# Gates of half of the tokens through an indirect scatter into DRAM, in place of one-hot products, and four more early chunks

## The chip, the cores and the metric

One core of one Trainium2 chip. The metric is the device time of one execution in microseconds, as the median of three runs.

## The reference

Two transformer-like blocks over 256 tokens of width 1024, all in float32. The change touches the last stage of the second block only, a product-key expert layer (`_peer`):

```python
q = (tok @ w_q).reshape(n_tok, 8, 2, 128)
s = jnp.einsum('nhpc,hpkc->nhpk', q, sub_keys)            # 8 heads, 2 halves, 128 keys
s_top, i_top = lax.top_k(s, 16)
cand = (s_top[:, :, 0, :, None] + s_top[:, :, 1, None, :]).reshape(n_tok, 8, 256)
best, pos = lax.top_k(cand, 16)
expert = ...                                              # i_top[.., 0, ..] * 128 + i_top[.., 1, ..] at pos
gate = jax.nn.softmax(best, axis=-1)
act = gelu(einsum('tkd,td->tk', u_emb[expert], tok)) * gate
out = einsum('tk,tkd->td', act, v_emb[expert])
```

There are 16384 experts, 128 x 128, and each token picks 128 of them (8 heads, 16 each; one expert can be picked by several heads, and its gates add up). The kernel doesn't gather: it computes the products with all experts and multiplies by a gate that is zero where an expert was not picked.

## The kernel before

Weights stream from HBM through a ring of four slots (`ring`, 512 KB each), loaded by SP. For float32 accuracy each weight chunk and each activation is kept as a high and a low part; ACT makes the high part (`take_hi`, `mid_hi`), DVE or POOL the low part (`take_lo`), and PE does three products (high x high, high x low, low x high; `TERMS`).

The expert layer (`peer`) takes the 16384 experts as 128 chunks of 128. A chunk is one second-half key j with all 128 first-half keys i on the partitions. `gate_map` [128, 128 chunks, 256 tokens] holds for each chunk gelu(u . token), later times the gate.

- Scores: PE multiplies queries by sub-keys for both token blocks of 128 (L3125). DVE then searches the two blocks one after the other (L3237 to L3278: the top 16 of each half, the top 16 of the pairs, the ranks, and from them `sel`: first index, second index, gate). The softmax has its exponential on ACT (L3196) and ends on DVE (L3284, `picked`).
- Early stage (`peer_u_early`, `EARLY` = 40 chunks): meanwhile PE runs chunks with the general routine (L280), ACT makes the high parts (L257) and the gelus (L3171), POOL the low parts (L263). POOL also makes the low parts of the first two middle chunks. That is all that POOL does.
- Middle stage (`peer_u_mid`, `MID` = 88 chunks, steps s = 0 to 87). After chunk 0 PE waits for `picked` and turns `sel` (six transposes, L3148), and ACT copies the result to `sel_t` (L3198). From step 1 to 64 a group g = s - 1 of four tokens is spread: DVE makes the one-hot rows `gated_i` (one-hot of i times the gate, L3294) and `hot_j` (L3295), PE multiplies them, one product of 128x128 per token (L3159), which gives the gates of all experts for these tokens in PSUM. `apply` (L3301) multiplies the chunks that are already in `gate_map` by them; for the later chunks ACT writes the gates there (L3217), and when the gelu of such a chunk comes, it goes to `late_gelu` (L3209) for the tokens already spread and is multiplied in by DVE (`take_mid`, L3115). `gates_before(s)` says how many tokens that is. DVE makes the low part of chunk s + 1 in step s (L263).
- Value stage (`peer_v`, 128 chunks): ACT makes the high part of the values (L3353); DVE splits the gated gelu of the chunk into high (L3371) and low (L3373) and makes the low part of the values (L263); PE adds 12 products of 512 columns into four banks (L3400). Each chunk uses one of two buffers, so ACT and DVE wait for PE's chunk j - 2. In the end each half is normalised and stored.

Order is by semaphores only; each engine runs its own program in the order written.

## Time and profile before

| | us |
|---|---|
| median of 3 runs | 2210.54 |
| lowest, highest | 2210.38, 2211.09 |
| span of the profiled execution | 2207.3 |
| PE, DVE, ACT, POOL busy in it | 2164.7, 1632.3, 1043.3, 105.9 |
| early stage, PE | about 1424 to 1536 |
| middle stage, PE | about 1536 to 1844 |
| value stage, PE | 1845 to 2200 |

The time of the profiled execution itself isn't given, only its span, from its first to its last instruction; the median lies 3.2 us above. Times in the rows below are us from the span's start. A row of the timeline has start, duration, engine, line, operation, output<-inputs, count, and in brackets the idle time of the engine before it and what ended it. Queue names (SPq) are the issuing of DMAs.

### The profile page before, as it was taken

The numbers are of one execution on the slowest core, as the hardware profiler recorded it, in microseconds if no ns is written. First come the engines' busy times: TensorE is split into PE (matmuls) and PEld (weight loads), VectorE is DVE, ScalarE is ACT, GpSimd is POOL, SyncE is SP. The second block draws the span as 40 slices with busy tenths as digits, with TensorE's granted clock in tenths as the row PEclk, the third lists the DMA queues.
The fourth block names the chain that finished last, engine by engine and source line by source line (L and its number), as shares of the span: only waits on it lengthen the run. The fifth ranks groups of instructions, "written<-read, shape, count | busy, mean of one in ns | idle before, by whom it ended". The sixth has DMA issues, their size and how long they took to land. (4 is left out here: it accounts for less than half of the span.)

```text
span 2207.3 us, 46147 instructions
## 1 busy us (share of the span) xinstructions
PE 2164.7 (98%) x18208; PEld 2053.0 (93%) x18208; DVE 1632.3 (74%) x3097; ACT 1043.3 (47%) x1695; POOL 105.9 (5%) x46
## 2 busy tenths in 40 slices
PE   9999999999999999999899999998999999999998
PEld 9999989999999998999889989998999998778787
DVE  6665868765875687876686587799899966776666
ACT  5444555444544466554453355444444444333333
POOL 0000000000000000000000000297000000000000
PEclk9999999999999999999999999999999999999999
DMA  6563535564556443566332235555444455555554
GB/s 218 180 202 123 204 108 174 180 203 133 179 176 202 145 166 123 172 196 211 120 114 69 80 117 179 174 183 179 135 144 146 148 174 193 190 187 188 188 190 151
DMA packets 100061, 361.11 MB, mean 164 GB/s; under 512 B 11544, under 2 KB 15784, under 8 KB 99760
## 3 DMA queue, kind: packets, MB, share of 16 engines
...
q8 instruction: 128, 2.10, 0.4%
...
## 5 line engine op out<-in xcount | busy, mean ns | idle before, releaser
L1177 DVE TENSOR_TENSOR w_lo<-ring,w_hi 128x1024 fp32r<-128x1024 f32 (+1 forms) x301 | 393.4, 1309 | 185.9 <-ACT w_hi L923 185.3
L923 ACT ACTIVATE w_hi<-ring 128x1024 fp32r<-128x1024 f32 (+1 forms) x301 | 337.4, 1126 | 333.6 <-PE ps L551 321.4
L551 PE MATMUL ps<-x_hi,w_hi 128*128 128x272 f32 (+1 forms) x1608 | 460.2, 286 | 0.9 <-DVE x_lo L1248 0.6
L551 PE MATMUL ps<-x_hi,w_lo 128*128 128x272 f32 (+1 forms) x1608 | 457.9, 285 | 0.0
L551 PE MATMUL ps<-x_lo,w_hi 128*128 128x272 f32 (+1 forms) x1608 | 455.5, 283 | 0.0
L551 PEld LDWEIGHTS ps<-x_hi,w_hi 128*128 128x128 f32 x1608 | 302.1, 188 | 4.1 <-DVE w_lo L1177 1.4
L551 PEld LDWEIGHTS ps<-x_hi,w_lo 128*128 128x128 f32 x1608 | 302.1, 188 | 0.0
L551 PEld LDWEIGHTS ps<-x_lo,w_hi 128*128 128x128 f32 x1608 | 301.8, 188 | 0.2
L3353 ACT ACTIVATE v_gated_hi<-ring 128x1024 fp32r<-128x1024 f32 x128 | 135.9, 1062 | 216.3 <-PE ps L3400 216.3
L3400 PE MATMUL ps<-v_gated_hi,gated_gelu_lo 128*128 128x512 f32 x512 | 202.4, 395 | 0.0
L3141 PE MATMUL ps<-tok_hi,u_mid_hi 128*128 128x256 f32 x704 | 201.6, 286 | 0.6 <-POOL u_mid_lo L263 0.6
L3400 PE MATMUL ps<-v_gated_hi,gated_gelu_hi 128*128 128x512 f32 x512 | 201.7, 394 | 0.0
L3400 PE MATMUL ps<-v_gated_lo,gated_gelu_hi 128*128 128x512 f32 x512 | 200.8, 392 | 0.0
L551 PE MATMUL ps<-hidden_hi,w_lo 128*128 128x272 f32 (+1 forms) x704 | 200.1, 284 | 0.0
L551 PE MATMUL ps<-hidden_hi,w_hi 128*128 128x272 f32 (+1 forms) x704 | 199.1, 283 | 0.0
L551 PE MATMUL ps<-hidden_lo,w_hi 128*128 128x272 f32 (+1 forms) x704 | 199.1, 283 | 0.0
L3141 PE MATMUL ps<-tok_hi,u_mid_lo 128*128 128x256 f32 x704 | 195.6, 278 | 0.0
L3141 PE MATMUL ps<-tok_lo,u_mid_hi 128*128 128x256 f32 x704 | 195.4, 278 | 0.0
L263 DVE TENSOR_TENSOR v_gated_lo<-ring,v_gated_hi 128x1024 fp32r<-128x1024 f32 x128 | 156.9, 1226 | 34.4 <-ACT v_gated_hi L3353 34.4
L263 POOL TENSOR_TENSOR u_early_lo<-ring,u_early_hi 128x1024 fp32r<-128x1024 f32 x40 | 100.5, 2522 | 1430.8 <-ACT u_early_hi L257 1430.6
L3178 ACT ACTIVATE u_mid_hi<-ring 128x1024 fp32r<-128x1024 f32 x88 | 93.4, 1061 | 160.3 <-PE ps L3141 157.4
L263 DVE TENSOR_TENSOR u_mid_lo<-ring,u_mid_hi 128x1024 fp32r<-128x1024 f32 x86 | 105.4, 1226 | 40.8 <-ACT u_mid_hi L3178 39.3
...
## 6 DMA issues: line engine op xcount, KB each, us to landing
ring<-in_gate_up SPq DMA_DIRECT2D x173, 512.0 KB, 3.5
ring<-in_peer_v SPq DMA_DIRECT2D x128, 512.0 KB, 3.3
...
ring<-in_peer_u_mid SPq DMA_DIRECT2D x88, 512.0 KB, 3.3
ring<-in_w_in SPq DMA_DIRECT2D x46, 512.0 KB, 3.4
ring<-in_peer_u_early SPq DMA_DIRECT2D x40, 512.0 KB, 3.3
ring<-in_project SPq DMA_DIRECT2D x32, 512.0 KB, 4.1
ring<-in_da_qk SPq DMA_DIRECT2D x18, 512.0 KB, 4.8
```

The source lines that it names most:

```text
L263: eng.tensor_tensor(parts[1][:, slot % nparts, 0:w.cols], ring[:, slot, 0:w.cols], parts[0][:, slot % nparts, 0:w.cols].bitcast(F32), ALU. ...
L551: mm = nc.tensor.matmul(ps[:, bank, 0:ntok], parts[left][:, item % SLOTS, t * P:(t + 1) * P], rhs[right][:, k, 0:ntok], start=start and n ...
L923: A.activation(parts_of(n)[0][:, n % SLOTS, 0:width[n]], ring[:, n % SLOTS, 0:width[n]], ACT.Copy).then_inc(hi_done.sem, 1)
L1177: V.tensor_tensor(parts_of(n)[1][:, n % SLOTS, 0:width[n]], ring[:, n % SLOTS, 0:width[n]], parts_of(n)[0][:, n % SLOTS, 0:width[n]].bitca ...
L3141: mm = nc.tensor.matmul(ps[:, 4 + s % 4, 0:SEQ], mid_parts[left][:, s % 2, P * k:P * k + P], x_parts[right][:, k, :], start=(k == 0 and n ...
L3178: A.activation(mid_parts[0][:, s % 2, :], ring[:, s % SLOTS, 0:D], ACT.Copy).then_inc(hi_done.sem, 1)
L3353: A.activation(parts[0][:, slot % 2, :], ring[:, slot, 0:D], ACT.Copy).then_inc(hi_done.sem, 1)
L3400: mm = nc.tensor.matmul(ps[:, 2 * tb + hf, :], gated_gelu[left][:, b, P * tb:P * tb + P], parts[right][:, b, 512 * hf:512 * hf + 512], sta ...
```

## The change

The tokens of block 0 (`SCATTERED` = 128 of them) no longer go through the one-hot products; those of block 1 (`SPREAD` = 128) still do. So there are 32 groups in place of 64.

For block 0 there is a table of 16384 experts x 128 tokens, 8.4 MB, in DRAM (`far_gates`). It is first filled with zeros by 16 DMAs of 512 KB, which POOL issues after every second low part of the early stage. When both blocks are searched, DVE works out an element index (expert times 128 plus token) and the gate for each of the 128 picks; POOL issues one indirect DMA for each pick, which adds 128 gates (one per token, on the partitions) to the table, 4 bytes each, and waits for the landing after each head's 16. In the value stage SP loads for each chunk the 128x128 gates from the table (`far_in`, 64 KB), and DVE multiplies them into `gate_map` before it splits the chunk.

`EARLY` goes from 40 to 44 chunks, and `MID` from 88 to 84. Block 1 is scored first into PSUM (`SEARCHED`) and block 0 second; DVE's search itself is unchanged. After the search only `sel` of block 1 is turned. The diff, cut:

```diff
@@ -55,7 +55,7 @@
 NKEY = 128
-EARLY = 40
+EARLY = 44
 STAYING = 36
@@ -66,6 +66,10 @@
 RANKS = list(range(TOPK)) + [NARROW_AT * (TOPK // NARROW) + HALF_ROW, WHOLE, NARROW_AT] + [0] * 5
+TOKEN_COLUMN = TOPK + 3
+SPREAD = P
+SCATTERED = SEQ - SPREAD
+ZERO_PIECES = 16
@@ -3041,6 +3044,10 @@
     TERMS = ((0, 0), (0, 1), (1, 0))
+    SEARCHED = (1, 0)
+    far_gates = nc.dram_tensor("far_gates", (NKEY * NKEY * SCATTERED, 1), F32, kind="Internal").ap()
+    far_pieces = far_gates.rearrange("(n p c) o -> n p (c o)", n=ZERO_PIECES, p=P)
+    far_chunks = far_gates.rearrange("(j i t) o -> j i (t o)", j=NKEY, t=SCATTERED)
@@ -3083,23 +3090,30 @@
         mid_parts = [sb_in(build, "u_mid_hi", [P, 2, D], F32R), sb_in(build, "u_mid_lo", [P, 2, D + LINE // 4], F32R)[:, :, lo_behind:lo_behind + D]]
-        sel_t = sb_in(build, "sel_t", [P, 3, SEQ])
+        sel_t = sb_in(build, "sel_t", [P, 3, SPREAD])
         iota = sb_in(build, "iota", [P, P])
...
         gated_i = sb_in(build, "gated_i", [P, 2, 4, P])
-        late_gelu = sb_in(build, "late_gelu", [P, 2, SEQ])
+        late_gelu = sb_in(build, "late_gelu", [P, 2, SPREAD])
+        at = nc.sbuf_base
+        far_index = nc.alloc_sbuf_tensor_at("far_index", [P, SEL], U32, offset=at)
+        far_gate = nc.alloc_sbuf_tensor_at("far_gate", [P, SEL], F32, offset=at + 4 * SEL)
+        far_in = nc.alloc_sbuf_tensor_at("far_in", [P, SLOTS, SCATTERED], F32, offset=at + 8 * SEL)
+        zeros = hot_j[:, :, :, :].rearrange("p b n j -> p (b n j)")
         iota4 = iota[:, :].unsqueeze(1).broadcast_to([P, 4, P])
...
         (scored, score_kept, picked, exp_in, exp_out, sel_turned, sel_copied, mid_done, mid_gelu, mid_taken, hots, spread,
-         g_copied, g_applied) = flags("scored", "score_kept", "picked", "exp_in", "exp_out", "sel_turned", "sel_copied", "mid_done",
-                                      "mid_gelu", "mid_taken", "hots", "spread", "g_copied", "g_applied")
-        TG = SEQ // 4
+         g_copied, g_applied, far_landed, far_used) = flags("scored", "score_kept", "picked", "exp_in", "exp_out", "sel_turned", "sel_copied", "mid_done",
+                                      "mid_gelu", "mid_taken", "hots", "spread", "g_copied", "g_applied", "far_landed",
+                                      "far_used")
+        far_full = flags(*(f"far_full_{n}" for n in range(SLOTS)))
+        TG = SPREAD // 4
...
         def gates_before(s):
-            return min(4 * max(s - 1, 0), SEQ)
+            return min(4 * max(s - 1, 0), SPREAD)
@@ -3120,11 +3134,11 @@
         def experts_in_pe(pe):
-            for tb in range(2):
+            for at, tb in enumerate(SEARCHED):
                 for n in range(SETS):
-                    mm = nc.tensor.matmul(ps[:, 4 * tb + n // 4, NKEY * (n % 4):NKEY * (n % 4) + NKEY], q[:, n, P * tb:P * tb + P],
+                    mm = nc.tensor.matmul(ps[:, 4 * at + n // 4, NKEY * (n % 4):NKEY * (n % 4) + NKEY], q[:, n, P * tb:P * tb + P],
                                           keys[:, n, :], start=True, stop=True)
-                    if tb == 1 and n % 4 == 3 or n == SETS - 1:
+                    if at == 1 and n % 4 == 3 or n == SETS - 1:
                         mm.then_inc(scored.sem, 1)
@@ -3143,9 +3157,8 @@
                     pe.wait_ge(picked.sem, 1)
-                    for tb in range(2):
-                        for j in range(3):
-                            mm = nc.tensor.transpose(ps[:, 2 + tb, P * j:P * j + P], sel[:, tb, j, :], ident[:, :])
+                    for j in range(3):
+                        mm = nc.tensor.transpose(ps[:, 2, P * j:P * j + P], sel[:, 1, j, :], ident[:, :])
                     mm.then_inc(sel_turned.sem, 1)
@@ -3160,10 +3173,20 @@
         def experts_in_pool(pool):
-            for i, slot, _turn in grouped(pool, w.n, SLOTS):
-                take_lo(pool, w, u_parts, i, slot)
+            pool.wait_ge(v_step.sem, v_step.at(1))
+            for i in range(w.n):
+                take_lo(pool, w, u_parts, i, i % SLOTS)
+                if i % 2 and i // 2 < ZERO_PIECES:
+                    pool.dma_start(far_pieces[i // 2], zeros).then_inc(far_landed.sem, 16)
             for s in range(2):
                 take_lo(pool, wm, mid_parts, s, s)
+            pool.wait_ge(far_landed.sem, 16 * ZERO_PIECES)
+            pool.wait_ge(picked.sem, 2)
+            for hd in range(PH):
+                for n in range(TOPK * hd, TOPK * hd + TOPK):
+                    pool.indirect_dma_start(out=far_gates, out_offset=bass.IndirectOffsetOnAxis(ap=far_index[:, n:n + 1], axis=0),
+                                            in_=far_gate[:, n:n + 1], in_offset=None, compute_op=ALU.add).then_inc(far_landed.sem, 16)
+                pool.wait_ge(far_landed.sem, 16 * (ZERO_PIECES + TOPK * (hd + 1)))
@@ -3195,8 +3218,7 @@
             act.wait_ge(sel_turned.sem, 1)
-            A.activation(sel_t[:, :, :].rearrange("p j (b t) -> p b j t", b=2), ps[:, 2:4, 0:3 * P].rearrange("p b (j t) -> p b j t", j=3),
-                         ACT.Copy).then_inc(sel_copied.sem, 1)
+            A.activation(sel_t[:, :, :].rearrange("p j t -> p (j t)"), ps[:, 2, 0:3 * P], ACT.Copy).then_inc(sel_copied.sem, 1)
             for s in range(MID - 1):
@@ -3206,11 +3228,8 @@
                         act.wait_ge(mid_taken.sem, s - 3)
-                    last = A.activation(late_gelu[:, s % 2, 0:at], ps[:, 4 + s % 4, 0:at], ACT.Gelu)
-                    if at == SEQ:
-                        last.then_inc(mid_gelu.sem, 1)
-                if at < SEQ:
-                    A.activation(gate_map[:, EARLY + s, at:SEQ], ps[:, 4 + s % 4, at:SEQ], ACT.Gelu).then_inc(mid_gelu.sem, 1)
+                    A.activation(late_gelu[:, s % 2, 0:at], ps[:, 4 + s % 4, 0:at], ACT.Gelu)
+                A.activation(gate_map[:, EARLY + s, at:SEQ], ps[:, 4 + s % 4, at:SEQ], ACT.Gelu).then_inc(mid_gelu.sem, 1)
                 if 1 <= s <= TG:
@@ -3219,6 +3238,7 @@
             link = Chain(dve, v_step)
+            link(V.memset(zeros, 0.0))
             top4 = top[:, :, :].rearrange("p (h e) k -> p h e k", e=2)
@@ -3280,10 +3300,15 @@
             link(V.reciprocal(total[:, :, :], total[:, :, :]))
-            for tb in range(2):
-                last = V.tensor_tensor(sel[:, tb, 2, :].rearrange("p (h k) -> p h k", h=PH), best[:, tb, :, :],
-                                       total[:, tb, :].unsqueeze(2).broadcast_to([P, PH, TOPK]), ALU.mult)
-            last.then_inc(picked.sem, 1)
+            V.tensor_tensor(sel[:, 1, 2, :].rearrange("p (h k) -> p h k", h=PH), best[:, 1, :, :],
+                            total[:, 1, :].unsqueeze(2).broadcast_to([P, PH, TOPK]), ALU.mult).then_inc(picked.sem, 1)
+
+            link(V.scalar_tensor_tensor(out=row_f[:, :], in0=sel[:, 0, 1, :], scalar=float(NKEY), in1=sel[:, 0, 0, :], op0=ALU.mult, op1=ALU.add))
+            V.tensor_tensor(far_gate[:, :].rearrange("p (h k) -> p h k", h=PH), best[:, 0, :, :],
+                            total[:, 0, :].unsqueeze(2).broadcast_to([P, PH, TOPK]), ALU.mult)
+            V.tensor_scalar(far_index[:, :], row_f[:, :], float(INDEX_SCALE * SCATTERED), iota_k[:, TOKEN_COLUMN:TOKEN_COLUMN + 1], ALU.mult,
+                            ALU.add).then_inc(picked.sem, 1)
+            dve.wait_ge(far_landed.sem, 16 * ZERO_PIECES)
@@ -3331,7 +3356,14 @@
                 sp.dma_start(final_g, a["final_g"].rearrange("p (s c) -> p s c", s=SLOTS)).then_inc(loaded.sem, 16)
-                load_stage(sp, "peer_v")
+                sp.wait_ge(far_landed.sem, 16 * (ZERO_PIECES + SEL))
+                for i, slot, turn in grouped(sp, wv.n, SLOTS):
+                    if not early(i, SLOTS):
+                        sp.wait_ge(far_used.sem, i - SLOTS + 1)
+                    sp.dma_start(far_in[:, slot, :], far_chunks[i]).then_inc(far_full[slot].sem, 16)
+                    if not early(i, SLOTS):
+                        sp.wait_ge(lo_done.sem, i + (wv.first - SLOTS + 1))
+                        sp.dma_start(ring[:, slot, 0:D], wv.ap[i]).then_inc(ring_full[slot].sem, 16)
                 for tb in range(2):
@@ -3344,7 +3376,8 @@
                             act.wait_ge(mid_taken.sem, last - 3)
-                            A.activation(late_gelu[:, last % 2, :], ps[:, 4 + last % 4, 0:SEQ], ACT.Gelu).then_inc(mid_gelu.sem, 1)
+                            A.activation(late_gelu[:, last % 2, :], ps[:, 4 + last % 4, 0:SPREAD], ACT.Gelu)
+                            A.activation(gate_map[:, NKEY - 1, SPREAD:SEQ], ps[:, 4 + last % 4, SPREAD:SEQ], ACT.Gelu).then_inc(mid_gelu.sem, 1)
                         else:
@@ -3361,11 +3394,14 @@
             def experts_out_dve(dve):
-                for j, slot, _turn in grouped(dve, wv.n, SLOTS):
+                for j, slot, turn in grouped(dve, wv.n, SLOTS):
                     b = slot % 2
...
                     value = gate_map[:, bass.ds(j, 1), :].rearrange("p j t -> p (j t)")
+                    dve.wait_ge(far_full[slot].sem, turn * 16 + 16)
+                    V.tensor_tensor(value[:, SPREAD:SEQ], value[:, SPREAD:SEQ], far_in[:, slot, :], ALU.mult).then_inc(far_used.sem, 1)
+                    dve.wait_ge(far_used.sem, j + 1)
                     if not early(j, 2):
@@ -3571,7 +3607,8 @@
     out["ind"], out["ind_t"] = con(ind), con(ind.transpose(2, 1, 0))
-    out["ranks"] = con(np.broadcast_to(np.array(RANKS, np.float32), (P, len(RANKS))))
+    out["ranks"] = np.tile(np.array(RANKS, np.float32), (P, 1))
+    out["ranks"][:, TOKEN_COLUMN] = np.arange(P)
     out["iota_scaled"] = con(np.broadcast_to(np.arange(P, dtype=np.float32) / INDEX_SCALE, (P, P)))
```

## Rows read from the trace of the kernel before

**Rows 1.** The page's first lines: span and busy time of PE, DVE, ACT, POOL.
```profile
span 2207.3 us, 46147 instructions
PE 2164.7 (98%) x18208; PEld 2053.0 (93%) x18208; DVE 1632.3 (74%) x3097; ACT 1043.3 (47%) x1695; POOL 105.9 (5%) x46
```

**Rows 2.** Windows: busy PE, PEld, DVE, ACT, POOL, clock, DMA share, GB/s.
```profile
1424.50:1536.50 112.00, 109.65 (x960) 109.07 (x960) 110.56 (x395) 55.65 (x82) 98.69 (x40) 1.00 0.53 177
1551.40:1660.00 108.60, 108.60 (x959) 108.60 (x958) 98.22 (x240) 50.27 (x120) 0.00 (x0) 1.00 0.45 147
```

**Rows 3.** Chain that ended last, in order: start, us, work.
```profile
1546.19 4.29 PE ps L3141 x24
...
1776.63 2.74 PE ps L3141 x24
1780.27 63.43 PE ps L3141 x552
1845.45 354.29 PE ps L3400 x1530
```

**Rows 4.** Timeline of PE where the middle stage starts.
```profile
1536.55 0.38 PE L3141 MATMUL ps<-tok_hi,u_mid_hi 128*128 128x256 f32 x1 [0.64 <-POOL u_mid_lo L263]
...
1544.65 1.54 PE L3148 MATMUL ps<-ident,sel 128*128 128x128 f32 x6 [5.10 <-DVE sel L3284]
...
1551.12 0.36 PE L3141 MATMUL ps<-tok_hi,u_mid_hi 128*128 128x256 f32 x1
```

**Rows 5.** Window of line L3141 alone: PE, PEld busy, clock, DMA, GB/s.
```profile
1546.00:1551.00 5.00, 4.47 (x24) 4.28 (x24) 0.66 0.00 2
```

**Rows 6.** Timeline of POOL, ACT and SP's queue in the early stage.
```profile
1425.46 2.40 POOL L263 TENSOR_TENSOR u_early_lo<-ring,u_early_hi 128x1024 fp32r<-128x1024 f32 x1 [3.26 <-ACT u_early_hi L257]
...
1526.56 2.46 POOL L263 TENSOR_TENSOR u_early_lo<-ring,u_early_hi 128x1024 fp32r<-128x1024 f32 x1 [0.28 <-ACT u_early_hi L257]
...
1525.15 0.39 ACT L3171 ACTIVATE gate_map<-ps 128x256 f32 x1 [1.37 <-PE ps L280]
...
1416.38 0.33 SPq L3118 DMA_DIRECT2D iota<-in_iota_scaled  x1
```

**Rows 7.** DMA issues: count, KB each, median us from issue to landing.
```profile
ring<-in_peer_u_early SPq DMA_DIRECT2D x40, 512.0 KB, 3.3
...
out<-gate_map SPq DMA_DIRECT2D x2, 512.0 KB, 2.7
...
iota<-in_iota_scaled SPq DMA_DIRECT2D x1, 64.0 KB, 1.8
```

**Rows 8.** Timeline of DVE in the early stage, beside POOL.
```profile
1420.26 3.27 DVE L3237 MAX8 peer_top<-ps 128x8 f32<-128x128 f32 x16 [4.17 <-PE ps L3125]
...
1526.46 0.29 DVE L3271 TENSOR_TENSOR rank<-row_f,iota_k 128x128 f32<-128x128 f32 x1
...
1526.79 2.38 DVE L3272 SCALAR_TENSOR_TENSOR row_f<-rank,iota_k 128x128 f32<-128x128 f32 x1
```

**Rows 9.** Timeline of DVE and ACT in the middle stage.
```profile
1620.70 1.23 DVE L263 TENSOR_TENSOR u_mid_lo<-ring,u_mid_hi 128x1024 fp32r<-128x1024 f32 x1 [0.32 <-ACT u_mid_hi L3178]
1621.84 1.11 DVE L3294 TENSOR_SCALAR gated_i<-iota,sel_t 128x128 f32<-128x128 f32 x4
...
1803.47 1.23 DVE L263 TENSOR_TENSOR u_mid_lo<-ring,u_mid_hi 128x1024 fp32r<-128x1024 f32 x1 [1.16 <-ACT u_mid_hi L3178]
...
1802.38 1.06 ACT L3178 ACTIVATE u_mid_hi<-ring 128x1024 fp32r<-128x1024 f32 x1 [1.39 <-PE ps L3141]
1803.35 0.36 ACT L3209 ACTIVATE late_gelu<-ps 128x256 f32<-128x256 f32 x1
```

**Rows 10.** Timeline of DVE in the value stage.
```profile
1901.18 0.29 DVE L3371 CAST gated_gelu_hi<-gate_map 128x256 fp32r x1 [0.48 <-PE ps L3400]
1901.51 0.43 DVE L3373 TENSOR_TENSOR gated_gelu_lo<-gate_map,gated_gelu_hi 128x256 fp32r<-128x256 f32 x1
1902.17 1.23 DVE L263 TENSOR_TENSOR v_gated_lo<-ring,v_gated_hi 128x1024 fp32r<-128x1024 f32 x1 [0.23 <-ACT v_gated_hi L3353]
```

3 lines of the change are left out of this document (1 added, 2 removed).

## The prediction

> **What bounds the kernel now.** I read the page's busy shares first: PE (TensorE) is busy 2164.7 us of a span of 2207.3 us, so time can only leave with PE's work or with PE's few gaps [rows 1]. The windows then show an early stage with all engines at work, and a middle stage with PE 100% busy at full granted clock, DVE at 90% and POOL at nothing [rows 2]. The chain that ended last runs through PE all the way from 1546 us, its last piece being the 354.29 us of the value stage [rows 3]. Its starts give the prices: a middle chunk with its four one-hot products takes 3.63 us (1776.63 to 1780.27), one without them (63.43 us for 23 chunks) 2.757 us, so four one-hot products cost 0.876 us of PE. There are 64 such groups (256 tokens, four to a group).
>
> The one large gap of PE in these stages is at the seam. Chunk 0 of the middle stage is done about 1539.5 us. PE then idles 5.10 us for the selection from DVE, and chunk 1 takes 4.29 us in place of 2.74 because the granted clock is at the lower level behind the idle time (0.66 in 1546 to 1551) [rows 3 to 5].
>
> **Parts that shorten PE's path.** 32 of 64 groups of one-hot products go: 32 x 0.876 = 28.0 us. This needs nothing else to be late. DVE's one-hots and gating of those groups go too; they were beside PE.
>
> **The seam.** Four chunks move from the middle to the early stage. Their price is the same on both sides (40 early chunks take 112 us and PE is busy for 109.65 of them [rows 2], about 2.72 each), so the move pays only through the idle time. POOL makes the low part of every early chunk and now also issues 16 DMAs of zeros there, after each second chunk. POOL has 0.3 us of idle per chunk [rows 6], so 0.6 us per pair, and is ahead by 1.5 us (its result of 1529.02 is wanted at 1530.5, two chunks after PE's end of 1525.1 that let ACT's gelu go). The first DMA falls into the 3.26 us in which POOL waits anyway. With c the POOL time of one DMA, PE is delayed by 15 x (c - 0.6) - 1.5 us. No row has a DMA from POOL. The nearest rows are SP's issue of 0.33 us and POOL's own pass over 1024 columns, 2.4 us [rows 6]. Below nothing is excluded, since nothing is taken off POOL. I take c = 1.2 us, nearer to the first because POOL moves no data in it, and keep 0.33 and 2.4 for the range: the delay is 7.5 us, with bounds 0 and 25.5.
>
> Then: middle chunk 0 starts at 1536.55 + 4 x 2.72 + 7.5 = 1554.9, ends 1557.6; three transposes 0.8, chunk 1 2.7, one group 0.9; chunk 2 starts at 1562.1. Before it started at 1551.12 [rows 4], and four chunks fewer are left, worth 11.0: 1562.1 against 1562.1, a seam worth nothing. With c = 0.33 DVE sets it: the selection is there at 1544.6 (up to 1547 if POOL still works beside it), chunk 2 starts about 1555.3, 7 us gained; with c = 2.4 some 18 us are lost.
>
> DVE gains three operations there (index, gate and scaled index of the other tokens) between the selection and the one-hots. DVE's two-input operations show two durations, 0.29 and 2.38 us, the second when POOL works [rows 8], so these three cost 0.8 to 7.2 us. They end by 1554, before PE ends chunk 0 and ACT has copied the turned selection (2.5 us of wait on DVE now). If POOL is fast (c = 0.33) this cover is gone; that is in the 1555.3. The memset of zeros costs at most the 1.23 us of a 1024-column pass and lies in the 4.17 us that DVE waits for the first scores [rows 8]; behind it POOL starts 0.2 us later, before its own 3.26 us of idle time.
>
> The zero pieces write 8.4 MB beside the ring loads: 512 KB per 5.4 us on top of 177 GB/s at a DMA share of 0.53 [rows 2], some 280 GB/s and 0.84 in proportion. A ring load lands in 3.3 us [rows 7], while its slot is asked for some 8 us after its issue (three chunks). A piece as long as a load (3.3 us) still fits. Cost 0, at most 3 us.
>
> **The scatter.** After its last low part POOL waits for the second selection and issues 128 indirect DMAs, with a wait for landing after each 16. Nothing else is queued behind them on POOL. SP, however, waits for all of them before it loads the first gates, and value chunk 0 waits for those. POOL starts at about 1559. PE would reach the value stage at 1562.1 + 31 x 3.633 + 51 x 2.757 + 1.75 (the present gap for the turned tokens) = 1817.1, against 1845.45: 28.3 us earlier. The last landing must be 3.3 us before that (a 64 KB load 1.8 us [rows 7], product 0.29, cast 0.29, low part 0.43 and starts). So 255 us cover the scatter. Eight landing waits at 2.7 us (the store to HBM [rows 7]) are 22, which leaves 1.82 us for each DMA. The indirect DMA is bounded by the same rows, 0.33 and 2.4 us, and again I take 1.2: 154 + 22 = 176 us, hidden with 79 us to spare. The Trainium skill, "DMA: Bandwidth & Descriptors", section "Latency and other measured facts", gives about 1 us for the emission on GpSimd; by that alone the scatter would be an estimated 150 us. No row here shows it.
>
> Beside the scatter DVE has 0.32 us of idle time per chunk with one-hots, and the chain PE, ACT high part, DVE low part has 0.36 us left per chunk without them (PE's end near 1802.3, low part ready 1804.70, wanted 1805.06) [rows 9]. I allow 2 us for disturbance; bounds 0 and the second rival.
>
> The ACT side: a gelu of 256 columns (0.36 us) becomes two of 128 (about 0.5 together) in 51 chunks. ACT idles 1.39 us before its next high part, and DVE 1.16 [rows 9]; cost 0, no gain.
>
> **The value stage.** DVE gets one product of 128 columns per chunk, 0.29 us as the short operations of rows 8, and a wait for its end (0.04 us). In front of the cast DVE waits 0.48 us for PE, and before the low part 0.23 us for ACT [rows 10]. The new work starts when the previous low part ends and fits the first gap with 0.1 us over; the second gives 0.2 more. Nothing is late. If that cover failed, each 0.1 us would cost 12.8. SP's far load waits for DVE's product of the chunk four before, and the ring load queued behind it waits for the same chunk's low part, which comes later anyway. Cost 0.
>
> **Sum.** 2207.3 - 28.0 + 0 + 2 = 2181.3 us of span. The profiled execution's own time isn't given; the median of the three runs, 2210.54, lies 3.2 us above the span, so 2184.5 us.
>
> **Rivals.**
> 1. The scatter outlasts its cover. At x us per DMA the value stage is late by 128 x (x - 1.82), and the 26 us are gone at x = 2.02. At 2.2 us: 48 + 1.6 for the lower clock behind the idle time, 2234 us, slower. For it: POOL's own pass takes 2.4 us; 4-byte pieces are nowhere in the trace. Against: POOL has nothing else to do, and the cover is 255 us. The Trainium skill speaks against the change here ("SBUF — State Buffer", the box on DVE blocking DMA): a DVE operation in a two-port mode keeps GpSimd from writing descriptors. By that rule the four one-hot scalings, 1.1 us of each 3.63 [rows 9], would take some 34 us from the cover and leave 1.55 us per DMA, still enough. No row shows it. Chance 0.15, 0.10 of it slower.
> 2. POOL's DMAs hold up DVE as its passes do now. Rows 8 show a two-input operation stretched by 2.09 us. With POOL issuing 90% of the time, each such operation would wait half of a DMA, 0.55 us; three per chunk with one-hots are 1.6, less 0.3 of slack, 1.3 x 31 = 40 us, and 22 further chunks lose 0.2 each: 45 us, 2184.5 - 2 + 45 = 2227.5 us, slower. It decides from 0.9 us of loss per one-hot chunk. Against: the stretched operations stand beside a POOL pass that streams 1024 columns, which a DMA issue doesn't. Chance 0.15, 0.09 slower.
> 3. The 16 zero DMAs starve PE in the early stage, c = 2.4: 2184.5 + 18 = 2202.5 us, faster still. Chance 0.07.
> 4. It doesn't do what it says: the 512-byte and 4-byte pieces crowd the ring loads, and the value stage's loads land late by 0.2 us a chunk: +25 us, 2209.5. Chance 0.03.
>
> **How the numbers follow.** The forecast of 2184.5 us, with 2177 to 2192 by c and the allowance, has 0.60. The range goes from 2173 (c = 0.33, no disturbance: 2175.5, less a little) to 2230, which takes in rivals 2 to 4 and the first half of rival 1. Slower by over 0.2% (what a measurement can tell here): 0.10 + 0.09 + 0.01 = 0.20; within it 0.06, from the middles of rivals 1, 2 and 4; faster 0.74.
>
> **What would show it.** The one-hot products are half as many, and chunk starts go from 3.63 to 2.76 us apart after 31 of them. The idle time of PE before the three transposes is gone. POOL's pairs of low parts stand 2 x 2.4 + c apart. POOL's last landing lies well before 1814 us and SP's first far load is not waited for; PE's gap before the value stage stays 1.75 us. A gap there that names the far loads is rival 1; DVE durations of 0.5 us and more above 1.23 in the middle stage are rival 2. The forecast is wrong if an indirect DMA takes over 1.8 us of POOL.

## The result and the profile after

The changed kernel takes 2226.61 us (median of 4 runs, 2224.38 to 2227.86) against 2210.72 us of the kernel before on the same chip (2210.38 to 2211.09). The ratio is 1.0073, with a 95% interval of 1.0062 to 1.0085: slower by 0.7%. The forecast was 2184.5 us, so the direction was wrong; 2226.61 us lies inside the range only because the range reached into the first rival, that the scatter outlasts its cover. That rival is what happened.

The page of the kernel after, its first lines and its group of the indirect DMAs (busy, mean ns of one, then the idle time before them):

```profile
span 2224.6 us, 46255 instructions
PE 2139.0 (96%) x17949; PEld 2026.0 (91%) x17949; DVE 1594.3 (72%) x3028; ACT 1037.4 (47%) x1682; POOL 359.4 (16%) x194
...
L3187 POOL DMA_INDIRECT far_gates<-far_gate,far_index x128 | 235.5, 1840 | 69.4 <-issue 45.5
```

PE lost 25.7 us of busy time (2164.7 to 2139.0, [rows 1]) and the span grew by 17.3 us all the same, so PE is idle for 43 us more than before. POOL, 5% busy before, has 235.5 us of indirect DMAs, 1.84 us each on average.

The end of the chain that ended last, in order of time (start, us, work), to be held against [rows 3]:

```profile
1845.94 1.54 POOL far_gates L3187
1853.33 2.98 DMA far_gates<-far_gate,far_index
1856.33 1.86 DMA far_in<-far_gates
1860.58 356.50 PE ps L3436 x1530
```

Before, this chain was PE alone from 1546 us on. Now it runs through POOL's scatter and through the first load of gates, and the value stage starts at 1860.58 in place of 1845.45.

Where PE and DVE waited, from the timelines (start, us, engine, line, operation, with the idle time before it in brackets):

```profile
1815.81 1.91 PE L3427 MATMUL ps<-ident,h 128*128 128x128 f32 x16
1860.58 0.77 PE L3436 MATMUL ps<-v_gated_hi,gated_gelu_hi 128*128 128x512 f32 x1 [42.86 <-DVE v_gated_lo L266]
```

```profile
1858.22 0.29 DVE L3403 TENSOR_TENSOR gate_map<-gate_map,far_in 128x128 f32<-128x128 f32 x1 [44.48 <-DMA far_in<-far_gates]
```

PE was done with the middle stage and its transposes at 1817.7 us and would have gone on there; the prediction had 1817.1. The ledger in spans: the value stage could have begun 1845.45 - 1817.7 = 27.8 us earlier than before; DVE's 44.48 us of waiting for the gates cost PE 42.86 us; the value stage itself takes 356.50 in place of 354.29 us, 2.2 more, since the clock granted behind the idle time is lower, as the windows show (busy time of PE, PEld, DVE, ACT and POOL, the clock, the DMA share, GB/s):

```profile
1800.00:1850.00 50.00, 17.67 (x153) 17.24 (x151) 7.42 (x11) 10.59 (x23) 36.59 (x23) 0.70 0.39 74
1850.00:1900.00 50.00, 39.42 (x163) 31.51 (x164) 31.12 (x61) 13.80 (x13) 4.26 (x3) 0.85 0.54 162
```

Together 42.9 + 2.2 - 27.8 = 17.3 us, which is the growth of the span. So the saving in one-hot products came in full, and more than all of it went into one wait.

### The profile page after: what moved, and what is told of

Read it like the earlier page. It is cut to its first block and busy times, and to the rows that moved or that the text cites. A ratio compares the mean times of both kernels' runs of the same rounds, so it can differ in the third digit from the quotient of the medians.

```text
span 2224.6 us, 46255 instructions
## 1 busy us (share of the span) xinstructions
PE 2139.0 (96%) x17949; PEld 2026.0 (91%) x17949; DVE 1594.3 (72%) x3028; ACT 1037.4 (47%) x1682; POOL 359.4 (16%) x194
## 5 line engine op out<-in xcount | busy, mean ns | idle before, releaser
L266 POOL TENSOR_TENSOR u_early_lo<-ring,u_early_hi 128x1024 fp32r<-128x1024 f32 x44 | 110.0, 2514 | 1424.0 <-DVE hot_j L3241 1417.4
L3187 POOL DMA_INDIRECT far_gates<-far_gate,far_index x128 | 235.5, 1840 | 69.4 <-issue 45.5
L3436 PE MATMUL ps<-v_gated_hi,gated_gelu_hi 128*128 128x512 f32 x512 | 202.3, 395 | 42.9 <-DVE v_gated_lo L266 42.9
L3155 PE MATMUL ps<-tok_hi,u_mid_hi 128*128 128x256 f32 x672 | 190.8, 284 | 0.7 <-POOL u_mid_lo L266 0.6
L3155 PE MATMUL ps<-tok_hi,u_mid_lo 128*128 128x256 f32 x672 | 187.1, 278 | 0.0
L3155 PE MATMUL ps<-tok_lo,u_mid_hi 128*128 128x256 f32 x672 | 187.0, 278 | 0.0
L3436 PEld LDWEIGHTS ps<-v_gated_hi,gated_gelu_hi 128*128 128x128 f32 x512 | 96.7, 189 | 72.8 <-issue 43.5
```

The lines of the kernel that those rows point to most:

```text
L266: eng.tensor_tensor(parts[1][:, slot % nparts, 0:w.cols], ring[:, slot, 0:w.cols], parts[0][:, slot % nparts, 0:w.cols].bitcast(F32), ALU. ...
L3155: mm = nc.tensor.matmul(ps[:, 4 + s % 4, 0:SEQ], mid_parts[left][:, s % 2, P * k:P * k + P], x_parts[right][:, k, :], start=(k == 0 and n ...
L3187: pool.indirect_dma_start(out=far_gates, out_offset=bass.IndirectOffsetOnAxis(ap=far_index[:, n:n + 1], axis=0), in_=far_gate[:, n:n + 1], ...
L3436: mm = nc.tensor.matmul(ps[:, 2 * tb + hf, :], gated_gelu[left][:, b, P * tb:P * tb + P], parts[right][:, b, 512 * hf:512 * hf + 512], sta ...
```

## Why the scatter is slow: what the trace of the kernel after shows

The 128 indirect DMAs start at 1557.06 and the last one ends at 1854.87, 297.8 us. By the rows of POOL this splits into four parts: 128 x 1.54 = 197.1 us at the duration that most of them have; 38.4 us above that, nearly all in 41 of them that last over 2 us; 45.5 us of "issue" gaps (0.30 us in front of nearly each, and a few pauses of 2 to 5.6 us); and 16.8 us in 7 waits for a landing.

POOL and DVE in a stretch of plain middle chunks, those without one-hot products:

```profile
1732.29 1.71 POOL L3187 DMA_INDIRECT far_gates<-far_gate,far_index  x1 [2.24 <-DMA far_gates<-far_gate,far_index]
1734.30 2.50 POOL L3187 DMA_INDIRECT far_gates<-far_gate,far_index  x1 [0.30 <-issue]
1737.11 2.42 POOL L3187 DMA_INDIRECT far_gates<-far_gate,far_index  x1 [0.30 <-issue]
1739.83 2.49 POOL L3187 DMA_INDIRECT far_gates<-far_gate,far_index  x1 [0.30 <-issue]
```

```profile
1734.16 1.23 DVE L266 TENSOR_TENSOR u_mid_lo<-ring,u_mid_hi 128x1024 fp32r<-128x1024 f32 x1 [1.38 <-ACT u_mid_hi L3201]
1736.88 1.23 DVE L266 TENSOR_TENSOR u_mid_lo<-ring,u_mid_hi 128x1024 fp32r<-128x1024 f32 x1 [1.29 <-ACT u_mid_hi L3201]
1739.68 1.23 DVE L266 TENSOR_TENSOR u_mid_lo<-ring,u_mid_hi 128x1024 fp32r<-128x1024 f32 x1 [1.37 <-ACT u_mid_hi L3201]
```

Compare starts and ends. Each DMA starts 0.14 to 0.23 us after DVE has begun its low part and ends 1.41 to 1.43 us after that pass has ended (1736.88 + 1.23 = 1738.11; 1737.11 + 2.42 = 1739.53). I sorted all 128 by where this pass stood when they started. Of 51 that started inside a pass, 41 took over 2 us, and the others had begun late in it, too late to be held for long. Of 35 during which a pass began, and 42 that overlapped none, not one took over 1.66 us. So one sentence describes them all: a DMA ends 1.54 us after its start, or 1.42 us after the end of the pass into which it started, whichever is later. No one of the 128 is off that by more than 0.12 us. Most of what is left comes from DVE's shorter operations: seven DMAs that started 0.18 to 0.20 us before the end of one (`gated_i`, or the product of `gate_map` with `late_gelu`) ended 1.41 us after it and lasted 1.59 to 1.62 us.

The same lines show why this is not an occasional loss. A held DMA ends 1.42 us after a pass, the next begins 0.30 us later, 1.72 us after the pass. The next pass begins 2.757 - 1.23 = 1.53 us after the end of the last. So the next DMA again starts about 0.2 us inside a pass, and so do all that follow: the two engines lock, one DMA to a chunk of 2.757 us instead of one in 1.845 us. A landing wait or a pause breaks the lock, and once a pass that came 0.3 us later than the others did (at 1723.11 us); then it forms again. In the chunks with one-hot products a chunk takes 3.63 us and two undisturbed DMAs 3.69, and there the lock is rare.

Two theories were to be told apart. A: DVE's low part, as an operation with two inputs, holds POOL's DMA. B: the ring loads, which go on in the same stretch, hold it. And beside them a question of bookkeeping: is the long scatter the whole of the loss?

## The experiments

Where not said otherwise the runs were taken beside the kernel before, at 2209.31 us (the first four), 2210.33 (the next four), 2209.68 (e10_pool_loads) and 2210.08 (the last three). A kernel with one run is compared with others only where they are 10 us and more apart, except where the text says so. Runs of different groups stand beside each other below; their kernels before differ by up to 1.4 us.

**Half of the picks scattered.**

```
-            for hd in range(PH):
+            for hd in range(PH // 2):
...
-                sp.wait_ge(far_landed.sem, 16 * (ZERO_PIECES + SEL))
+                sp.wait_ge(far_landed.sem, 16 * (ZERO_PIECES + SEL // 2))
```

> Only the picks of heads 0 to 3 are added to the table (64 indirect DMAs in place of 128); the gates of the other four heads are left out for these tokens, everything else is as in the changed kernel. Theory A (the 42.9 us that PE idles ahead of the value stage are the scatter's end and nothing else): 64 DMAs end near 1557 + 150 = 1707 us, the value stage starts at 1817.5 as PE's work allows, and the time is 2226.6 - 43.1 - 2.2 (value chunks at the lower clock behind the idle time) = 2181.3 us. Rival B (the table costs in another way too: the far loads, the DMA traffic or DVE's product slow the value stage, so that a wait of some 10 us or more stays): 2190 us or more.

Measured: 2189.1 us (2186.16 to 2190.53), ratio to before 0.9904 (0.9888 to 0.9921). With 64 DMAs the scatter was over near 1690 us, long before it was wanted, and 37.5 us went. That is the loss of 15.9 us and a saving of 21.6 besides: the length of the scatter is what makes the change slow. It is not 2181.3 us, though. The value stage began at 1823.77 rather than 1817.7, and SP's queue and DVE show why:

```profile
1809.43 4.35 SPq L234 DMA_DIRECT2D ring<-in_peer_v  x4
1813.83 0.57 SPq L3358 DMA_DIRECT2D ring<-in_final_g  x1
1814.44 8.12 SPq L3363 DMA_DIRECT2D far_in<-far_gates  x5
```

```profile
1821.41 0.29 DVE L3403 TENSOR_TENSOR gate_map<-gate_map,far_in 128x128 f32<-128x128 f32 x1 [8.12 <-DMA far_in<-far_gates]
```

The first load of gates is 64 KB and took 1.86 us in the kernel after, where SP's queue stood empty. Here it is issued at 1814.44 behind four ring loads and one of the final scales, 2.5 MB, and DVE can use it only 7 us later. The part of the rival that said the loads of gates come late was right, at 6 us.

**The ring loads of the middle stage made thin.** Each loads 64 columns instead of 1024 from the fifth middle chunk on; the other columns of those chunks are not loaded.

```
+                sp.dma_start(ring[:, slot, 0:64], wm.ap[i][:, 0:64]).then_inc(ring_full[slot].sem, 16)
```

> In the middle stage the ring loads bring 64 of the 1024 columns (the rest of each weight chunk is stale, so those gelus are wrong); DVE, ACT, PE and POOL do all that they did. 49 of the 128 indirect DMAs last 2.4 to 2.5 us in place of 1.54. Theory A (DVE's low part holds what POOL needs): the long ones stay, some 49, and the value stage starts within 3 us of 1860.6 us. Rival B (the ring loads' traffic in the DMA engines holds them up): the long ones are gone in the middle stage, the scatter takes 128 x 1.845 + 20 = 256 us, and the value stage starts at 1817.5 to 1822 us.

Measured: 2223.08 us, 39 DMAs over 2 us (the changed kernel has 41, not the 49 of the expectation), 36.9 us above 1.54 us in all; value stage from 1857.24, 3.3 us earlier. The windows of 1680 to 1800 us show how much traffic went, first in the changed kernel, then here (columns as above; the last two are the DMA share and GB/s):

```profile
1680.00:1800.00 120.00, 119.97 (x1043) 119.77 (x1043) 61.47 (x87) 60.46 (x130) 98.37 (x44) 1.00 0.70 190
```

```profile
1680.00:1800.00 120.00, 119.97 (x1045) 119.77 (x1044) 61.89 (x88) 60.37 (x130) 98.07 (x45) 1.00 0.21 13
```

With 13 GB/s in place of 190 POOL is as busy as before, and the scatter takes 294.2 us in place of 297.8. B falls.

**The low part of the plain chunks over 64 columns**, the rest left out.

```
+                        V.tensor_tensor(mid_parts[1][:, (s + 1) % 2, 0:64], ring[:, (s + 1) % SLOTS, 0:64],
+                                        mid_parts[0][:, (s + 1) % 2, 0:64].bitcast(F32), ALU.subtract).then_inc(lo_done.sem, 1)
```

> In the middle chunks without one-hot products DVE makes the low part of 64 columns only (the other 960 stay stale), some 0.2 us in place of 1.23; the ring loads are whole. Theory A (DVE's two-input pass holds POOL's DMA): the 49 long DMAs fall to 1.54 us, 45 us less; the scatter ends about 1812 and the value stage starts at 1818 to 1823 us. Rival B (ring loads): the long ones stay, the value stage starts near 1860 us.

Measured: 2193.99 us. The group of the DMAs on the page:

```profile
L3187 POOL DMA_INDIRECT far_gates<-far_gate,far_index x128 | 201.0, 1570 | 70.1 <-issue 45.1
```

201.0 us of DMA time for 235.5, 3 DMAs over 2 us for 41, the gaps as before. Value stage from 1827.58: the scatter, begun at 1557.99, ends at 1822 and still comes last, by some 10 us. The expectation of 1818 to 1823 was too early for that.

**The low part replaced by a sum over one input**, of the same 1024 columns and the same length; it leaves the low part out.

```
+                            V.tensor_reduce(mid_parts[1][:, (s + 1) % 2, 0:1], ring[:, (s + 1) % SLOTS, 0:D], AX.X, ALU.add).then_inc(lo_done.sem, 1)
```

> In the same chunks DVE's low part is replaced by a sum over the 1024 columns of the ring slot: as long a pass (about 1.15 us) but with one input from SBUF (the low part is not made). If it is the second SBUF input that holds POOL, as the Trainium skill has it (SBUF — State Buffer, Who interferes with whom), the long DMAs are gone and the value stage starts at 1818 to 1823 us. If any DVE pass of that length holds POOL, the long ones stay and it starts near 1860 us.

Measured: 2193.45 us, value stage from 1827.77, 4 DMAs over 2 us, none of them beside a sum. DVE and POOL in the same stretch as above:

```profile
1737.36 1.22 DVE L3339 TENSOR_REDUCE u_mid_lo<-ring 128x1 fp32r<-128x1024 f32 x1 [1.30 <-ACT u_mid_hi L3201]
```

```profile
1736.05 1.54 POOL L3187 DMA_INDIRECT far_gates<-far_gate,far_index  x1 [0.30 <-issue]
1737.89 1.54 POOL L3187 DMA_INDIRECT far_gates<-far_gate,far_index  x1 [0.31 <-issue]
1739.74 1.54 POOL L3187 DMA_INDIRECT far_gates<-far_gate,far_index  x1 [0.30 <-issue]
```

The second of these starts 0.53 us inside DVE's pass. By the sentence above it would be held until 1738.58 + 1.42 = 1740.00 and last 2.11 us; it takes 1.54. Of the 28 DMAs that started inside such a sum and nothing else of DVE's, 25 of them with over 0.2 us of it left, not one took over 1.55 us. An equally long pass with one input doesn't hold it; one with two inputs does.

The sum differs in a second thing: it writes one column where the low part writes 1024, so this pair alone would leave the writing as a rival. DVE's product of the one-hot results speaks against that. It reads `gate_map` from SBUF and its other input from PSUM, and writes all its columns to SBUF. Two lines of the changed kernel, DVE and then POOL:

```profile
1598.05 0.37 DVE L3326 TENSOR_TENSOR gate_map<-gate_map,ps 128x220 f32<-128x220 f32 x1
```

```profile
1598.14 1.54 POOL L3187 DMA_INDIRECT far_gates<-far_gate,far_index  x1 [0.30 <-issue]
```

This DMA started 0.29 us before the end of the product and, held like the others, would last 1.71 us; it takes 1.54. In all runs together 59 DMAs started over 0.05 us after the start of such a product and over 0.2 us before its end, and none took over 1.56 us. The product with `late_gelu`, whose two inputs are both in SBUF, did hold: the ten DMAs that started over 0.05 us after its start and over 0.15 us before its end lasted 1.58 to 1.65 us and ended 1.41 to 1.42 us after it. So it is the second input from SBUF, as far as passes this short can show it; no run has a pass of 1024 columns that reads one input and writes them all.

The Trainium skill ("SBUF — State Buffer", section "Who interferes with whom") says that a DVE instruction with two SBUF inputs contends with a GpSimd instruction that reads SBUF, and one with a single input outside the two-port modes doesn't: the pair of runs agrees with that. The same section infers that such a tensor_tensor leaves descriptor writing on GpSimd alone. The measurement decides against it for this indirect DMA: 2.42 to 2.50 us beside the pass, 1.54 us without.

**The low part in two passes of 512 columns**, which computes the same.

```
-                    take_lo(dve, wm, mid_parts, s + 1, (s + 1) % SLOTS)
+                    dve.wait_ge(hi_done.sem, s + 1 + (wm.first + 1))
+                    for half in range(2):
+                        part = slice(D // 2 * half, D // 2 * half + D // 2)
+                        last = V.tensor_tensor(mid_parts[1][:, (s + 1) % 2, part], ring[:, (s + 1) % SLOTS, part],
+                                               mid_parts[0][:, (s + 1) % 2, part].bitcast(F32), ALU.subtract)
+                    last.then_inc(lo_done.sem, 1)
```

> DVE makes the low part of each middle chunk in two passes of 512 columns (about 0.69 us each) in place of one of 1024 (1.23 us); nothing else is changed. Theory A (an indirect DMA that starts while DVE's two-input pass runs waits for the end of that pass, and as both have a period of 2.76 us it meets every pass): a DMA now waits at most half a pass, and the lock step of the two is broken; of the 45 us of stretched DMAs some 15 stay, the scatter ends 30 us earlier and the value stage starts at 1825 to 1840 us. Rival (what counts is DVE's total time with two inputs in a chunk): the same 45 us, value stage near 1860 us.

Measured: 2196.37 us, 3 DMAs over 2 us, 7.4 us above 1.54 in all, value stage from 1829.26. The edit splits the passes of all middle chunks, those with one-hot products too. DVE's work is nearly the same (1.29 us for both halves against 1.23), but a DMA is now let go between the halves or after the second, none lasts over 2.08 us, and the lock doesn't form. It gives 30.2 of the 33 us that leaving out the pass gave (2226.61 - 2196.37, against 32.6 and 33.2). In this kernel some DMAs meet another two-input operation, the one-hot rows `hot_j` (0.68 us): four that started inside it lasted 1.90 to 2.08 us.

**The zeros on SP's queue** in place of POOL's, still 44 early chunks.

```
+                if i % 2 and i // 2 - 2 < ZERO_PIECES:
+                    sp.dma_start(far_pieces[i // 2 - 2], zeros).then_inc(far_zeroed.sem, 16)
...
-                if i % 2 and i // 2 < ZERO_PIECES:
-                    pool.dma_start(far_pieces[i // 2], zeros).then_inc(far_landed.sem, 16)
```

> The 16 zero pieces are issued by SP behind its ring loads of the early stage, no longer by POOL; nothing else is changed. DVE's search ends at 1555.5 us in the changed kernel, 10.9 us later than before, with one two-input operation of 12.65 us. Theory A (the zero DMAs fill the 0.3 us that POOL idled after each low part, in which DVE got its turn): the search ends at 1544 to 1547 us again, PE's idle time of 4.8 us before the transposes is gone, and the scatter starts at 1551 to 1553 in place of 1557.1 us. The value stage still waits for the scatter and starts some 5 us earlier, near 1856 us. Rival B (the traffic of the zeros slows the search or the early stage): the search ends near 1555 us as now.

Measured: 2222.81 us. The first half of the search is as fast as before the change, as expected, but the scatter starts at 1559.7, 2.7 us later than with the zeros on POOL, where 1551 to 1553 was expected. The next section reads this one together with the following.

**40 early chunks instead of 44**, as before the change, the zeros on POOL.

```
-EARLY = 44
+EARLY = 40
```

> EARLY back to 40, all else as in the changed kernel. Theory A (the time is set by the scatter, and the scatter by the end of the search): the search ends within 3 us of 1555.5, PE idles some 15 us there, and nothing of it is seen in the end, since the scatter ends as it did: value stage at 1853 to 1863 us. Rival (the four early chunks carry some of the time): the time rises by the extra idle time of 11 us.

Measured: 2212.88 us, one run; selection at 1544.82 and not at 1555, scatter from 1546.68, still 43 DMAs over 2 us, value stage from 1846.08. The expectation that the number of chunks leaves the selection where it was is wrong.

**Three edits together**: 40 early chunks, zeros on SP, the low part in two passes; and the final scales loaded behind the first gates.

> All together: EARLY = 40, the zeros on SP, the low parts of the middle stage in two passes, and SP loads the first far gates ahead of the final norm's weights. Theory A: scatter from 1547 us for 265 us (128 x 1.845, seven landing waits, pauses) if nothing is stretched, 15 us more for what the two passes leave; PE reaches the value stage at 1816.5 us by its own work. Value stage at 1817 to 1832 us, time 2182 to 2197 us, against 2210.7 before and 2226.6 with the change. Rival (splitting doesn't help): value stage near 1855 us, 2220 us.

Measured: 2192.47 us (2191.55 to 2192.87), ratio 0.9918 (0.9902 to 0.9935), faster than both kernels. The scatter has landed by 1813, yet the value stage starts only at 1824.31. DVE's wait:

```profile
1821.95 0.29 DVE L3414 TENSOR_TENSOR gate_map<-gate_map,far_in 128x128 f32<-128x128 f32 x1 [5.75 <-DMA far_in<-far_gates]
```

As with half of the picks, the first gates stand behind the ring loads of the value stage in SP's queue; to take the final scales out from between them didn't cure it.

**The first gates loaded by POOL**, right behind its own last landing wait, with 40 early chunks and the split low part, zeros on POOL. As in the kernels before, the low parts of all middle chunks are split, not only those of the plain ones.

```
+            for i in range(SLOTS):
+                pool.dma_start(far_in[:, i, :], far_chunks[i]).then_inc(far_head[i].sem, 16)
```

> 40 early chunks, the low part of the plain middle chunks in two passes of 512 columns, zeros on POOL as in the changed kernel, and the first four loads of gates issued by POOL right behind its last landing wait, not by SP behind the ring loads of the value stage. In e9_all_40 the scatter had landed about 1813 us, the first load of gates then took 5.41 us on SP's queue behind three ring loads, and PE stood idle for 4.3 us before a value stage that began at 1824.31. Theory A (the place in SP's queue costs it): POOL's loads take about 2 to 3 us each, DVE doesn't wait for them, the value stage begins at 1819 to 1821, and the time is 2187 to 2189 us. Rival B (the DMA engines themselves are full of ring loads, whatever the queue): POOL's first load lands as late as SP's, 5 us and more after its issue, value stage from 1823 to 1825, 2191 to 2193 us. The seam should be that of e7_early_40: selection at 1544.8, scatter from 1546.7; by both theories fewer than 10 of the 128 indirect DMAs take over 2 us.

Measured: 2194.8 us (2192.09 to 2197.1), ratio 0.9936 (0.9919 to 0.9952). DVE no longer waits for the gates, as theory A has it, but the time is neither theory's: the selection came at 1551.75 where 1544.8 was expected, and everything behind it 7 us later. The value stage began at 1826.72. Two operations of DVE in the first half of the search tell of it; this is the second:

```profile
1479.95 12.64 DVE L3299 TENSOR_TENSOR apart<-peer_idx_f,rank 128x2048 f32<-128x2048 f32 x1
```

**The same with the zeros on SP**, that is e9_all_40 with the first gates on POOL.

> e9_all_40 (40 early chunks, zeros on SP's queue, low parts of the plain middle chunks in two passes) with the first four loads of gates issued by POOL right behind its last landing wait. In e10_pool_loads DVE no longer waited for those loads, but a search that ended 7 us late (one two-input operation of DVE's first half took 12.64 us beside POOL's passes and zero DMAs) moved everything behind it. Theory A: with the zeros on SP that operation takes 4.4 us, the selection is there at 1545.2 and the value stage begins at 1820, PE's idle time before it under 2 us; time 2187 to 2189 us, with a spread of the runs under 2 us. Rival B: with the late selection gone the DMA engines or POOL's queue become late instead, and the value stage begins at 1823 to 1825: 2191 to 2193 us.

Measured: 2184.89 us (2183.94 to 2193.36, three of four within 2183.9 to 2185.0), ratio 0.9901 (0.9880 to 0.9922): the best of all. The fourth run, 8 us longer, is against the expected spread of under 2 us, and its cause is open. The expected 2187 to 2189 us was a little high, by the value stage (354.24 us for 357.27 in e9_all_40), which I had not taken to be shorter without an idle time in front of it: the clock granted from 1800 to 1850 us is 1.00 here and was 0.93 there. The end of its chain, DVE's first use of the gates, and the same operation of the search:

```profile
1804.45 14.15 PE ps L3165 x120
1818.60 1.75 PE ps L3444 x16
1820.35 354.24 PE ps L3453 x1530
```

```profile
1475.50 4.41 DVE L3305 TENSOR_TENSOR apart<-peer_idx_f,rank 128x2048 f32<-128x2048 f32 x1
...
1816.71 0.29 DVE L3420 TENSOR_TENSOR gate_map<-gate_map,far_in 128x128 f32<-128x128 f32 x1 [0.16 <-DMA far_in<-far_gates]
```

PE goes from the middle stage through its transposes into the value stage without a gap, as in the kernel before [rows 3]. Issued by POOL at 1814.62, the first gates are in use at 1816.71, 2.1 us later; on SP's queue behind the ring loads it took 5.41 us.

It is not the queue of its own that does it, though. SP issued one ring load at 1812.72 and the next three from 1815.54 on, so POOL's first load stands 0.9 us ahead of those three, where in e9_all_40 it stood behind them. The four loads of POOL, issued at 1814.62, 1815.21, 1815.77 and 1816.30, landed 2.06, 4.00, 4.88 and 5.90 us later. The page of the profile has their median:

```profile
far_in<-far_gates POOLq DMA_DIRECT2D x4, 64.0 KB, 4.4
```

The last two, which ran beside the three ring loads, took as long as those on SP's queue in e9_all_40 (5.41, 5.12, 4.80 and 4.44 us). In e10_pool_loads, where all four were issued before the next ring load (1822.15), they took 2.25 to 2.97 us. So rival B is right in its mechanism: beside the ring loads a load of gates is late on either queue. What the edit gains is that the first gates are issued earlier, ahead of them. A kernel in which SP itself issues the gates ahead of the ring loads wasn't run.

**40 early chunks once more**, the kernel of e7_early_40 unchanged.

> The kernel of e7_early_40 word for word (the changed kernel with 40 early chunks), again and with more runs. e10_pool_loads had the same seam but for nothing that touches it, and its search ended at 1551.75 where that of e7_early_40 ended at 1544.8. Theory A (with the zeros on POOL the long wait of one DVE operation comes or stays away from one execution to the next): the runs spread over 4 us or more, 2212 to 2220 us, and the profiled one shows either an operation of 12.6 us and a scatter that starts near 1553, or 4.4 us and 1546.7. Rival B (the long wait is fixed by the program): all runs within 2 us of 2212.9.

Measured: 2216.87 us (2213.44 to 2221.15, 6 runs), ratio 1.0031 (1.0018 to 1.0044); in the profiled run the operation took 12.66 us, the selection came at 1549.04 and the scatter began at 1550.91. So the single run of e7_early_40 was a lucky one. Theory A holds in its spread (7.7 us): the same program showed 4.41 us in one profiled execution and 12.66 us in the other. They ran on two chips, so whether the execution or the chip decides isn't separated; nor did the scatter start as late as the 1553 us expected.

**40 early chunks and zeros on SP**, the low part in one pass.

> The changed kernel with 40 early chunks and the zeros on SP's queue; only the number of early chunks separates it from e4_zeros_on_sp (selection 1553.8, scatter from 1559.7, 2222.8 us). Theory A (the early chunks by themselves hold up the end of the search, by ACT's exponential behind their copies and by POOL's later passes): selection at 1545.2 as in e9_all_40, scatter from 1547.1, about 40 of its DMAs over 2 us, value stage from 1846, 2212 to 2214 us. Rival B (only the zeros on POOL did the harm, the number of chunks does nothing): 2220 us and more.

Measured: 2212.74 us, one run; selection at 1545.30, scatter from 1547.21, 41 DMAs over 2 us, value stage from 1845.34. Theory A.

## The seam: two causes that hid each other

The kernel after and the runs that differ from it in the early chunks and in the queue of the zeros make a table; in it stand the moment at which the selection is ready and the time.

| | zeros on POOL | zeros on SP |
|---|---|---|
| 44 early chunks | 1555.19; 2226.61 us | 1553.80; 2222.81 us |
| 40 early chunks | 1544.82 and 1549.04 (and 1551.75 in e10_pool_loads); 2212.88 and 2216.87 us | 1545.30; 2212.74 us |

One cause is a starved DVE. POOL and DVE of the kernel after in the first half of the search:

```profile
1477.13 0.57 POOL L3180 DMA_DIRECT2D far_gates<-hot_j  x1
1477.72 4.76 POOL L266 TENSOR_TENSOR u_early_lo<-ring,u_early_hi 128x1024 fp32r<-128x1024 f32 x2
1482.42 0.57 POOL L3180 DMA_DIRECT2D far_gates<-hot_j  x1
1483.01 4.77 POOL L266 TENSOR_TENSOR u_early_lo<-ring,u_early_hi 128x1024 fp32r<-128x1024 f32 x2
1487.72 0.57 POOL L3180 DMA_DIRECT2D far_gates<-hot_j  x1
1488.32 3.88 POOL L266 TENSOR_TENSOR u_early_lo<-ring,u_early_hi 128x1024 fp32r<-128x1024 f32 x1
```

```profile
1477.29 12.65 DVE L3296 TENSOR_TENSOR apart<-peer_idx_f,rank 128x2048 f32<-128x2048 f32 x1
```

A direct DMA costs POOL 0.57 us, less than half of the 1.2 us that I took. But it fills the time in which POOL stood idle between two passes, and DVE's operation, 2.29 us when alone, gets in only at 1487.65, after four passes of POOL. In the kernel before it took 4.40 us, one pass of waiting. The windows show the idle time that went, first after, then before (columns as above; POOL's busy time is the fifth of the busy times):

```profile
1450.00:1500.00 50.00, 48.58 (x423) 48.02 (x423) 49.42 (x100) 24.34 (x36) 49.62 (x27) 1.00 0.84 277
```

```profile
1450.00:1500.00 50.00, 48.25 (x423) 47.87 (x422) 49.35 (x173) 23.97 (x35) 45.71 (x19) 1.00 0.55 185
```

Of nine profiled kernels with the zeros on POOL eight show 12.64 to 12.67 us there; of the four with the zeros on SP none does (4.41 us). In return the POOL pass at 1488.32 takes 3.88 us in place of 2.4: the two hold each other.

The other cause is ACT's exponential for the second half of the search, which stands in ACT's program behind the work of the last early chunks. ACT and DVE in e4_zeros_on_sp:

```profile
1552.53 0.42 ACT L3225 ACTIVATE best<-best 128x256 f32<-128x256 f32 x1
```

```profile
1542.02 2.29 DVE L3304 TENSOR_REDUCE sel<-apart 128x128 f32<-128x2048 f32 x1
...
1553.05 0.42 DVE L3307 TENSOR_REDUCE peer_total<-best 128x16 f32<-128x256 f32 x1 [8.74 <-ACT best L3225]
```

Here the search ended at 1544.3, 1 us later than before the change, and DVE then waited 8.74 us for ACT. Four more early chunks push this exponential back by 11 us (1537.77 before, 1548.77 after). In e4_zeros_on_sp it comes another 3.8 us later (1552.53), which neither of the two causes accounts for. POOL's rows name a candidate: four passes of the last early chunks take 13.28 us in place of some 9.7, beside two of DVE's wide two-input operations (from 1532.94 and 1537.59 us), which in the kernel after come 10 us later and miss those passes. That this is the reason is read from the trace, not tested.

```profile
1533.30 13.28 POOL L266 TENSOR_TENSOR u_early_lo<-ring,u_early_hi 128x1024 fp32r<-128x1024 f32 x4 [0.54 <-ACT u_early_hi L260]
```

In the kernel after both are late at the same time, and neither cure alone shows what it is worth: the zeros on SP gain 1.4 us at the selection with 44 chunks, 40 chunks gain 3 to 10 us with the zeros on POOL, and both together gain 9.9 us, the same in all three kernels that have both (1545.16 to 1545.30). In time, 44 chunks cost 2222.81 - 2212.74 = 10.1 us with the zeros on SP, single runs both, 3.8 us of delayed exponential and 4 us of an unexplained pause (below) included.

Why does a late selection cost that much, when PE has four chunks more to work on meanwhile? Because the scatter is what ends last. With the zeros on SP it starts 12.5 us later with 44 chunks (1559.72 against 1547.21), 8.5 of them from the selection and 4 from a longer pause before the first DMA that the trace names "issue"; it takes as long (291.6 and 292.5 us), and the value stage starts 11.5 us later. If the scatter were hidden, 44 chunks might be worth something: PE reached the value stage at 1817.7 in the kernel after and at 1820.35 in e11_best, which differ in other edits too. I haven't run the combination that would have both.

## The prediction, point by point

- *32 groups of one-hot products go, 28.0 us.* Right. Half of the products are gone (PE has 256 of these instructions left of 512, two to a token), chunk starts go from 3.63 to 2.757 us apart, and PE was through at 1817.7 against 1817.1.
- *The seam is worth nothing.* The sum came out (chunk 2 at 1561.89, forecast 1562.1), by luck: the reasons did not. (109.65 / 40 is 2.74 us for an early chunk, not 2.72, which moves nothing.) I let POOL's DMAs delay PE by 7.5 us; they cost 0.57 us each and delayed it not at all. Instead the selection was 11 us late. I had the rows for this and read them one way only: rows 8 show a two-input DVE operation stretched by a POOL pass, and rows 6 that POOL has 0.3 us of idle per chunk. DVE gets its turn in just that idle time, and I gave it away to the DMAs and counted only what that does to PE. For ACT's exponential I had no term: of the steps that move with four chunks it is the one that I didn't list.
- *The zero pieces fit beside the ring loads, cost 0.* Right; that window shows a DMA share of 0.84 and 277 GB/s, put at 0.84 and 280, and PE is as busy as before.
- *The scatter: 1.2 us per DMA, 176 us in all.* This is the step that failed. I took the value near SP's issue of 0.33 us because POOL moves no data. Measured were 1.54 us undisturbed, a gap of 0.30 us which I had not put in at all, 9.8 us in three pauses, and 38.4 us of holds: 297.8 us in place of 176. The sign that I had named for a wrong forecast, over 1.8 us of POOL for an indirect DMA, is there: the mean is 1.84. The point from which it costs was given as 2.02 us for each DMA, landing waits apart; (297.8 - 16.8) / 128 is 2.20. Without the holds it is 1.90, over the 1.82 that the cover allows, and e5_short_low shows just that, a value stage from 1827.58 and still 15 us faster than before.
- *The estimate by the Trainium skill* ("DMA: Bandwidth & Descriptors", section "Latency and other measured facts"), 1 us for an emission, was too low here: 1.54 us and the gap of 0.30 were measured. By the rule on two-port modes in the Trainium skill ("SBUF — State Buffer", the box on DVE blocking DMA) the one-hot chunks should have cost an estimated 34 us. Nothing of that size is seen: in those chunks nearly all DMAs take 1.54 us, and the few that started shortly before the end of a scaling at most 1.62. What held the 41 DMAs agrees with the other rule of the same page of the Trainium skill (section "Who interferes with whom"), on two SBUF inputs. The hold itself stands in rows 8, which I had read as something that befalls DVE beside a POOL pass; in the rows above POOL's DMA waits for a pass of DVE.
- *Rival 1* was priced at 2234 us for 2.2 us per DMA and came in at 2226.6: of the 7.4 us between, 1.9 are the earlier start of the scatter (1557.1 for 1559), 2.2 the landings (16.8 in the seven waits and 2.98 for the last, for 22), and 2 the allowance for disturbance, of which nothing was needed; 1.3 stay unassigned. Its mechanism (POOL's own cost) was half of it; the lock with DVE was in no rival. I gave rival 2 to the same pair of engines, but with DVE as the one that loses. DVE's low part still takes 1.23 us.
- *The value stage: one product more per chunk, hidden.* Right. It takes 0.29 us, PE is busy without a gap from 1870 to 2190, and the value stage takes 354.24 us in e11_best against 354.29 before.
- *SP's far loads, cost 0.* Wrong for the first of them: behind the ring loads they made PE idle for 4.3 us (e9_all_40) and 6.5 us (e1_half_picks), seen as soon as the scatter is out of the way.
- The forecast of 2184.5 us is near what e11_best measures, 2184.89 us. The sum of the parts was about right for a kernel in which the scatter is hidden; that it would be hidden was the error. The last tenths are luck: e11_best has 40 early chunks, its value stage begins at 1820.35 us and not at 1817.1, and its profiled execution took 1.8 us more than its span and not 3.2.
